# Two scans of gated recurrences: keys folded into the exponents, queries in 64x256, sums copied to PSUM

## What is computed

```
f = lb + (1 - lb) * sigmoid(z);  logf = log(max(f, 1e-30));  k = (1 - lb) * sigmoid(-z)
diff   = b_t - b_s                       # b: running sum of logf
scores = sum_k q[t,k] * k[s,k] * exp(b_t[k] - b_s[k])      for s <= t
o      = scores @ v + (q * exp(b_t)) @ state
```

## Time and profile before

| | us |
|---|---|
| median of 3 runs | 3473.53 (3471.25 to 3475.16) |
| profiled execution, from its first to its last instruction | 3475.4 |
| mixer's quick phase, layer 2 (its products) | about 1810 to 1978 |
| attention, layer 2 | 1980 to 2040 |
| scan, layer 2; layer 3 | 2040 to 2205; 2874 to 3037 |

### The profile page before, as it was taken

How to read it: one execution, slowest core, us unless ns; L and a number is a source line. 1 busy time by engine, 2 the same in 40 slices (tenths; PEclk the granted TensorE clock), 3 DMA queues, 4 the chain that set the end, 5 groups by cost and what they waited for, 6 DMA issues and landing times.

```text
span 3475.4 us, 44870 instructions
## 1 busy us (share of the span) xinstructions
PE 3315.4 (95%) x16138; PEld 2538.4 (73%) x16138; DVE 2112.2 (61%) x3509; ACT 969.1 (28%) x2203; POOL 1588.7 (46%) x1534
## 2 busy tenths in 40 slices
PE   8989999999999999999999988999999987899998
PEld 5665555555557967888888756688888865678887
DVE  7577756544544296555646668478764776656554
ACT  2076211001021174211122264222213244332211
POOL 1054322222235224444454467456645547655654
PEclk9999999999999999999999989999999998999999
DMA  7300223333312201345432200244443200022222
GB/s 254 130 10 7 97 98 120 104 122 114 107 58 73 79 2 37 122 158 170 158 96 85 64 12 11 85 156 158 153 143 99 86 28 18 12 88 88 88 89 79
DMA packets 91129, 317.87 MB, mean 91 GB/s; under 512 B 10816, under 2 KB 13152, under 8 KB 90912
## 3 DMA queue, kind: packets, MB, share of 16 engines
q1 hardware_dynamic: 64224, 218.34, 19.5%
q10 hardware_dynamic: 24768, 90.19, 7.1%
q0 software_dynamic: 1920, 6.49, 0.7%
HBM read 312.88 MB, written 2.10 MB: 91 GB/s over the span
## 4 chain that ended last, share of the span: by engine, by line
PE 86%; DVE 7%; ACT 3%; POOL 2%; issue 2%; DMA 0%; DVEq 0%; ACTq 0%; SPq 0%; POOLq 0%
PE ps L1336 66%; PE ps L1338 4%; PE ps L631 3%; PE ps L1293 2%; PE ps L1006 1%; PE ps L1246 1%; PE ps L992 1%; PE ps L1028 1%; PE ps L1189 1%; DVE arena L2626 1%; PE ps L1231 1%; PE ps L1064 1%; ACT arena L1520 1%; DVE arena L2584 1%; PE ps L1261 1%
## 5 line engine op out<-in xcount | busy, mean ns | idle before, releaser
L1336 PE MATMUL ps<-arena 128*128 128x256 f32 (+1 forms) x3744 | 952.4, 408 | 0.2
L1336 PEld LDWEIGHTS ps<-arena 128*128 128x128 f32 x3744 | 710.8, 190 | 204.9 <-issue 1.7
L2757 POOL TENSOR_TENSOR arena<-ring,arena 128x512 f32<-128x512 f32 (+1 forms) x140 | 182.6, 1304 | 836.8 <-PE ps L1336 836.8
L1336 PE MATMUL ps<-arena,ring 128*128 128x256 f32 (+1 forms) x2032 | 524.9, 410 | 3.1 <-ACT arena L1690 3.1
L1336 PE MATMUL ps<-hbuf,ring 128*128 128x256 f32 (+1 forms) x1824 | 469.4, 407 | 4.2 <-ACT hbuf L1797 1.2
L1336 PEld LDWEIGHTS ps<-arena,ring 128*128 128x128 f32 x2032 | 385.3, 190 | 119.5 <-ACT arena L1690 5.9
L1336 PEld LDWEIGHTS ps<-hbuf,ring 128*128 128x128 f32 x1824 | 345.8, 192 | 113.7 <-ACT hbuf L1797 19.5
L2300 DVE TENSOR_TENSOR arena<-ps,arena 128x256 f32<-128x256 f32 (+1 forms) x192 | 86.1, 449 | 356.7 <-PE ps L1336 235.6
L2187 DVE CUSTOM_DVE_ANT_0 aring<-aring,csil,adab 128x1024 f32<-128x1024 f32 x176 | 261.7, 1508 | 1.8
L2305 DVE SCALAR_TENSOR_TENSOR resid<-ps,mod,resid 128x256 f32<-128x256 f32 (+2 forms) x296 | 137.4, 482 | 185.2 <-PE ps L1336 180.5
L2740 POOL TENSOR_TENSOR arena<-ring 128x512 f32<-128x512 f32 (+1 forms) x140 | 182.1, 1301 | 141.2 <-PE ps L1336 133.6
(11 more groups left out here) (324 smaller groups left out, 5342.3 us busy)
## 6 DMA issues: line engine op xcount, KB each, us to landing
aring<-in_ada ACTq DMA_DIRECT2D x172, 512.0 KB, 4.7
ring<-in_mlp SPq DMA_DIRECT2D x128, 512.0 KB, 3.7
ring<-in_up SPq DMA_DIRECT2D x88, 512.0 KB, 3.3
ring<-in_in SPq DMA_DIRECT2D x56, 512.0 KB, 3.3
ring<-in_down SPq DMA_DIRECT2D x32, 512.0 KB, 3.6
ring<-in_odd_in SPq DMA_DIRECT2D x24, 512.0 KB, 3.3
arena<-in_ada SPq DMA_DIRECT2D x16, 512.0 KB, 13.7
ring<-in_out SPq DMA_DIRECT2D x16, 512.0 KB, 3.3
```

Source lines behind the costliest of these rows:

```text
L1336: return nc.tensor.matmul(ps[:, bank, 0:p.tw], w, x, start=start, stop=stop, skip_group_check=True)
L2757: nc.gpsimd.tensor_tensor(s[3], f0[:, h:2 * h], s[1], ALU.subtract).then_inc(wsum_ready, 1)
```

## The change

It multiplies by the keys before the exponential, as a sum of logarithms. In the mixer DVE clamps the keys at 2^-120; GpSimd splits them in two factors, ACT takes two logarithms and GpSimd adds them (six blocks a layer, iterations 5 to 10). In attention DVE adds or subtracts the running sums, `sum_keys`, six times. In the scan the exponentials then give weighed keys, and `weigh_levels` and the key half of `weigh_ends` go away. For u >= 1 the differences read the running sums from a copy in PSUM bank 7 that ACT makes (`copy_sums`); the early parts use bank 5 alone from the third on. Queries are laid out so that 14 products of 64x256 do for 28. ACT's level_decays(u+1) and copy_sums(u+2) stand behind take_pairs(u), ahead of keep_early and take_levels(u); the first unit's order changes too.

```diff
-        EARLY_BANK = (5, 7, 5, 7, 5, 7, 5, 7)
+        EARLY_BANK = (5, 7, 5, 5, 5, 5, 5, 5)
+        SUM_BANK = 7
...
                             if li == 0:
-                                pe.wait_ge(level_weighed, 2 * blk + d + 1)
+                                pe.wait_ge(level_decay, 2 * blk + d + 1)
...
-                        pe.wait_ge(early_taken, r - 1)
+                        pe.wait_ge(early_taken, r - 1 if m == 2 else r)
...
+                def log_keys(b):
+                    act.wait_ge(keys_clamped, 6 * mixer_phases.index(i) + b + 1)
+                    nc.scalar.activation(log_key(b), log_key(b), ACT.Ln)
+                    nc.scalar.activation(log_key_low(b), log_key_low(b), ACT.Ln).then_inc(keys_logged, 1)
...
                     if n < N:
                         keep_u3(n)
+                    if i in mixer_phases:
+                        for b in LOGS.get(n, ()):
+                            log_keys(b)
...
                     act.wait_ge(cumulated, 6 * n + u + 1)
+                    act.wait_ge(keys_summed, 6 * n + u + 1)
+                    plain, of = ((QF, src), (KF, keys))[d]
+                    nc.scalar.activation(plain[:, d, :].rearrange("p (t k) -> p t k", t=4), of, ACT.Exp)
                     for t in range(4):
+                        if d == 0:
+                            nc.scalar.activation(KF[:, d, t * P:(t + 1) * P], keys[:, t, :], ACT.Exp, bias=e[:, t, 128:129])
+                        else:
+                            nc.scalar.activation(QF[:, d, t * P:(t + 1) * P], src[:, t, :], ACT.Exp, scale=-1.0, bias=e[:, t, 128:129])
...
+                def copy_sums(u):
+                    if u >= 6:
+                        return
+                    b, d = u // 2, u % 2
+                    act.wait_ge(level_diff, 6 * n + u)
+                    act.wait_ge(early_taken, KT * n + 2)
+                    act.wait_ge(cumulated, 6 * n + u + 1)
+                    nc.scalar.activation(ps[:, SUM_BANK, :].rearrange("p (t k) -> p t k", t=4), E[:, 3 * d + b, :, 1 - d:129 - d],
+                                         ACT.Copy).then_inc(sums_copied, 1)
...
                 end_decays(0)
+                keep_early(EARLY_AT[0, "ends"][0:1])
+                level_decays(0)
                 end_queries(0)
-                keep_early(EARLY_AT[0, "ends"][0:1])
+                keep_early(EARLY_AT[0, "ends"][1:2])
+                copy_sums(1)
                 end_decays(1)
-                keep_early(EARLY_AT[0, "ends"][1:2])
-                level_decays(0)
                 keep_early(EARLY_AT[0, "ends"][2:])
                 for u in range(6):
                     take_pairs(u)
+                    level_decays(u + 1)
+                    copy_sums(u + 2)
                     keep_early(EARLY_AT.get((u, "levels"), ()))
                     take_levels(u)
-                    level_decays(u + 1)
                     end_queries(u + 1)
                     end_decays(u + 2)
...
+                        if p >= 3 and p % 2:
+                            sum_keys(layer - 2, (p - 3) // 2)
...
-                nc.vector.tensor_scalar(KR[:, b, :], KR[:, b, :], OMLB[:, b:b + 1], None, ALU.mult)
+                chain(nc.vector.tensor_scalar(KR[:, b, :], KR[:, b, :], OMLB[:, b:b + 1], KEY_TINY, ALU.mult, ALU.max))
...
+                    sums = src
+                    if u:
+                        dve.wait_ge(sums_copied, 5 * n + u)
+                        sums = ps[:, SUM_BANK, :].rearrange("p (t k) -> p t k", t=4)
                     for li, m in enumerate(LEVELS):
+                        bd = src[:, :, m - 1 + d:128:2 * m].unsqueeze(3).broadcast_to([P, 4, nb, m])
+                        bs = sums[:, :, m - 1 + d:128:2 * m].unsqueeze(3).broadcast_to([P, 4, nb, m])
+                        if d == 0:
+                            nc.vector.tensor_tensor(w[:, :, 0], bs, k[:, :, 0], ALU.add)
+                            nc.vector.tensor_tensor(w[:, :, 1], x[:, :, 1], bd, ALU.subtract)
+                        else:
+                            nc.vector.tensor_tensor(w[:, :, 0], bd, x[:, :, 0], ALU.subtract)
+                            nc.vector.tensor_tensor(w[:, :, 1], k[:, :, 1], bs, ALU.subtract)
...
-                    nc.vector.tensor_tensor(KF[:, d, :], KF[:, d, :], KR[:, 3 * d + b, :], ALU.mult)
...
-                def weigh_levels(u):
...
+                        for b in CLAMPS.get(n - 1, ()):
+                            pool.wait_ge(gate_clamped, 6 * mixer_phases.index(i) + b + 1)
+                            key = KR[:, b, :].rearrange("p (a t) -> p a t", a=2)
+                            nc.gpsimd.tensor_scalar(log_key_low(b), key, SPLIT, 1.0, ALU.mult, ALU.min)
+                            nc.gpsimd.tensor_scalar(log_key(b), key, 1.0 / SPLIT, 1.0, ALU.max, ALU.mult).then_inc(keys_clamped, 1)
+                        for b in LOGS.get(n - 1, ()):
+                            pool.wait_ge(keys_logged, 6 * mixer_phases.index(i) + b + 1)
+                            nc.gpsimd.tensor_tensor(log_key(b), log_key(b), log_key_low(b), ALU.add)
...
                             for hx in range(2):
                                 rows = slice(64 * hx, 64 * hx + 64)
-                                for half in range(2):
-                                    x = nc.gpsimd.tensor_tensor(dst[rows, half, hx], w[rows, 2 * half:2 * half + 2],
-                                                                q[rows, 2 * half:2 * half + 2], ALU.mult)
+                                x = nc.gpsimd.tensor_tensor(dst[rows, hx], w[rows], q[rows], ALU.mult)
```

55 lines of the change are left out of this document (33 added, 22 removed).

## The result

The changed kernel takes 3499.2 us in the median (3496.6 to 3501.7), beside 3474.4 us for the kernel before on the same chip: ratio 1.0069, 95% interval 1.0057 to 1.0081. It is slower by 0.7%, where I had forecast 17 us less, and 26 us above the upper end of my range. Its profiled execution took 3496.6 us with a span of 3494.7, against a span of 3475.4 before.

The account below looks back on a forecast made before the run. TensorE, busy 95% of the span, was taken as the bound. Units 15.0 plus scan starts 13.0, less mixer 7.0 and attention 4.0, gave 17.0 us less than the median 3473.5: 3456.5 us, range 3441 to 3473.

Parts of the forecast that it names:

- Differences: Scan, units u>=1: with one input in PSUM, 14 differences take 5.0 us a unit in place of about 8.8.
- a conflict left in full: Scan: upper bound if DVE still waits out GpSimd's longer queries, 0.95 us a difference, 13.3 us a unit.
- 15.0 for the units: Scan: units 1 and 3 fall to unit 5's length, 6.1 us less in layer 2 and 8.9 in layer 3.
- Weights: Scan: weighing by keys goes away; saving not added up, counted within unit lengths, worth nothing in units 2 and 4.
- Queries and ACT's order: Scan: queries, 10.2 us a unit instead of 13.0, off the path; ACT's new order just hidden, charged 0.5 to 0.8 us a unit.
- Start of a scan: Scan's start: ACT takes the early part sooner, so pairs(1) come 6.5 us earlier a scan, 13.0 in sum.
- Attention: Attention: six sum_keys a layer on DVE cost 4.0 us in all, bounds 2 and 7.
- The mixer: Mixer: GpSimd's clamps and additions stall TensorE 3.5 us a layer, cost 7.0 in all, bounds 4 and 11.
- clamps at 1.0: Mixer: 1.0 us a GpSimd clamp, with additions at 1.5, gives the upper cost bound of 11 us.
- (d): Rival, chance 0.07: scan conflict stays in full, differences take 0.95 us and delay take_levels; 18 us slower, 3491.
- stalls in the mixer above 5 us a layer: Mixer: one of the signs named in advance that would show the forecast wrong.

Follow-up runs that it names:

- e6: e5 without the copy of the sums to PSUM, so all differences of units 1 to 5 read two SBUF operands: 3463.2 us, ratio 0.9964.
- e14: e5 with differences read from SBUF and queries of 64x128, ACT's new order kept: one execution of 3456.8 us.
- e7: e5 with each level query made by four GpSimd instructions of 64x128 instead of two of 64x256: 3446.0 us, ratio 0.9920.
- e16: e5 with every scan part undone (SBUF differences, 64x128 queries, weighed levels, both old ACT orders); only end weights keep logarithmic keys: 3471.7 us, ratio 0.9987.
- e5: Changed kernel with one key logarithm a block, no GpSimd key clamps or key additions, constant restored in attention's key sums: 3449.0 us, ratio 0.9922.
- e10: e5 with VectorE multiplying the seven levels by the keys behind the exponential, as in the kernel before: 3473.6 us, ratio 0.9993.
- e15: e5 with SBUF differences, 64x128 queries and the old ACT order at the scan's start: one execution of 3469.0 us.
- e4: Kernel before the change plus each mixer's twelve GpSimd clamps as dead work, scan untouched: 3520.9 us, ratio 1.0137.
- e12: e5 with two dead GpSimd instructions of 128x512, of different operations, in each of six passes of a mixer: one execution of 3456.1 us.
- e2: Changed kernel with each GpSimd key clamp replaced in place by multiply, multiply by 1.0: 3466.0 us, ratio 0.9974.

## Why the prediction was wrong

**Differences.** Right. "14 x 0.36 = 5.0 us a unit": measured one every 0.33 us, and the slower start of 0.06 us that I had allowed for a PSUM operand isn't there (0.41 us with one, 0.42 with none). My bound for a conflict left in full, 0.95 us a difference beside the larger queries, is what e6 measured. I had 15.0 for the units and measured 17.0. Undoing the PSUM copy costs 14 us beside queries of 64x256, and 10.8 us in the units beside queries of 64x128 (e14 against e7, one profile each). The parts don't add up: the copy and the weighing, undone one at a time, cost 14 and 24.6 us, and all parts together 16.1 us in the units (e16 against e5). With either conflict left, units 1 and 3 stay long (e6: 27.0 and 24.5; e10: 28.3 and 27.2).

**Weights.** "in u=1 and 3 what is saved is only what stood before the merge of the unit; in units 2 and 4 ... worth nothing". Not contradicted for queries of 64x128: e16 puts the weighing back on top of e15 (with the old order in the units), and from pairs 1 to pairs 5 it takes 95.0 and 96.1 us beside 95.8 and 95.8. In the changed kernel it is worth 24.6 us (e10). I costed it by VectorE's busy time in the kernel before, not by what it would do beside the larger queries that the change brings; that the queries' size makes the difference is likely from the 6.26 against 4.63 us, but e10 and e16 differ in more than that.

**Queries and ACT's order.** "off the path at either bound" and "just hidden" are both confirmed: undone, neither makes it slower by more than 0.5 us, and the runs can't tell either from no change.

**Start of a scan.** 31.7 us after the scan's start were forecast for pairs(1); measured 31.4. Right in size, and that was luck. The reason I gave, ACT's order, explains some 1.2 of the 6.5 us when it is undone alone. The largest piece that the runs found is the 5.61 us addition, some 3 us of a start (e4: 41.09 against 37.98), which I had read in the earlier trace rows and not put in the sum by itself. It isn't firmly there even without the change: of the six starts with the old order and the weighing (before, e4, e16), four have it. The other 3 to 4 us are shared among parts that no run takes apart.

**Attention.** 4.0 forecast, 2.4 measured, inside my bounds of 2 and 7, but no more than the stage scatters between executions.

**The mixer.** This is the step that failed: "The first now gets four clamps in front: 4 x 0.8 (L2827, the nearest, takes 0.82 in attention) = 3.2, less the margin of 1.3: 1.9 us of stall." Three things are wrong in it.

First, the price. The earlier trace rows show a tensor_scalar of the same engine and size, but with two multiplications; the change's clamps hold a minimum and a maximum. I took the shape for the price. Among pairs the operation decides: 1.93 against 0.62 us (e12), in the same place some 2.05 against 0.70 (e2). The bound "clamps at 1.0" was half of what came.

Second, the passes. I charged the clamps only where they meet the logarithm additions. They stand in three passes a layer, two of them ahead of any addition. At 0.7 us these two nearly hide (e2: 12.09 and 12.68 us), at 2.05 they don't: 8.2 us against a room of 4.1. The room itself I had right, a margin of 1.3 us beside 2.5 us of additions is 3.8. The two passes with additions alone stand 1.6 us each, not 0.8: the four additions take 5.5 us there, not 5.0.

Third, the clock. TensorE's stalls are 18.2 us a layer, the loss 25.5. The earlier trace rows told that the granted clock was 0.50 behind an idle stretch, and I used that in the scan's start but not here. In layer 2 a stall of 4.0 us lengthened its pass by 5.7 to 6.0 us, one of 7.0 by 10.2; in layer 3 it was 5.9 and 7.1, and 9.3. Stalls of 1.6 us cost 1.8, at a clock of 1.00.

With the measured price and room the sum would have been: three stalls of 4.1, 4.1 and 7.1 us and two of 1.4 a layer, 36 us in place of 7, 3456.5 + 29 = 3486 us, and with the 15 us that the slower products took, 3501. It measured 3499.2. The rival on the slow side was the wrong one: (d) put the loss in the scan, and no rival had GpSimd's price in the mixer beyond 11 us. The sign was named, though: "stalls in the mixer above 5 us a layer". There were 18.2.

## What to carry to other kernels

Before an operation goes to another engine because that engine has room, find a row of the same operation on it, not only of the same shape; where there is none, let the upper bound be several times the nearest row (here it was 2.4 times). Where TensorE waits for a producer once in a short pass, write down the room of that producer in us (here 4.1 of 12.1), and add to a stall of several us what TensorE's lower clock takes afterwards (here nearly half as much again for stalls of 4 to 7 us). And an engine that is only shifted within its room can still hurt: moving GpSimd's sums by 4 us put them beside VectorE's taps, VectorE came late to the next pass, and that cost 14 us, though nobody waited for GpSimd. And what one part of a change is worth depends on the others: the weighing cost 24.6 us beside the new queries, and nothing that the runs can tell where the other parts were undone too.

## What the runs showed of the hardware

- GpSimd, tensor_scalar of 128x512 in fp32: 0.62 us for two multiplications or add and multiply, 0.78 for multiply and add, 1.93 for each of the four pairs with a minimum or maximum that were tried, 1.5 to 1.67 for a single operation, a multiplication too (e12). The Trainium skill's GPSIMD Engine Reference (4.1 "Engine selection") says of one-input elementwise work that it runs at roughly line rate on this engine; the trace agrees for the pairs of multiplications and additions (VectorE's own takes 0.43 us) and not for the single operations and the pairs with a minimum or maximum, which take 2.4 to 3.1 times the 0.62 us.
- VectorE's tensor_scalar of 128x512 takes 0.43 us alone, 0.7 to 0.76 beside GpSimd's clamps and 1.37 us beside GpSimd's tensor_tensor. The Trainium skill's SBUF — State Buffer ("Who interferes with whom") lets whoever issues first keep the shared port pair for its whole instruction, for VectorE in its two-port modes; 0.43 us plus most of a weight sum of 1.27 is what the trace shows; in which mode VectorE was, no view tells.
- With both operands in SBUF a difference of 128x256 takes 0.95 us beside 64x256 queries and 0.67 to 0.74 beside 64x128 ones; with one in PSUM it takes 0.41 beside either. The larger query is worse for a neighbour that reads SBUF; for the kernel it was 6 us a scan (e6, e14), of which a part may be the clock's.
- A GpSimd addition of 1.27 us was held for 5.56 us by a run of VectorE instructions that had no pause between them; in layer 3 of the same kernel it took 1.31 us beside such a run, and VectorE was the one held (e16).
